# A third token block's u products by rows, a shorter search, and sums held in PSUM in a product-key expert layer

## The chip, the core and the metric

The kernel runs on one core of a Trainium2 chip. The metric is the device time of one execution, in microseconds, as the median of the runs. The core has five engines that matter here: TensorE (PE, with its weight loads as PEld), VectorE (DVE), ScalarE (ACT), GpSimd (POOL) and SyncE (SP), which only issues transfers. 16 DMA engines serve them.

## The reference, cut to what matters

One decoder layer on 1024 tokens of width 1024 in float32. Attention and retention come first and give `h` after a layer norm. The change touches what follows, the product-key experts:

```python
q = (xt @ w_pq).reshape(T, H, 2, 128)              # H = 8 heads
s = einsum('thpd,hpkd->thpk', q, sub_keys)         # 2 x 128 scores a head
s1, i1 = top_k(s[:, :, 0], 16); s2, i2 = top_k(s[:, :, 1], 16)
cand = s1[..., :, None] + s2[..., None, :]         # 16 x 16 sums
top_s, pos = top_k(cand.reshape(T, H, 256), 16)
idx = 128 * i1 + i2 at pos                         # 128 experts a token
g = softmax(top_s)
a = gelu(einsum('cd,ced->ce', x, u[idx])) * g
y = einsum('ce,ced->cd', a, v[idx])
h = layer_norm(ALPHA * h + y, ln2_w, ln2_b)
```

There are 128 x 128 experts, so `u` and `v` have 16384 rows of 1024 numbers.

## The kernel before, in words

The tokens are eight blocks of 128. There are two ways to do the expert sums. **Dense:** multiply by all rows of `u` (or `v`) on TensorE, with a table of gates that is zero where an expert isn't chosen. **By rows:** gather the 128 chosen rows of each token with indirect transfers, and take dot products (`u`) or weighted sums (`v`) on VectorE. `UB = 2` blocks have `u` by rows, `GB = 2` blocks have `v` by rows; the others are dense. Each float32 product is three matmuls on split operands: hi x hi, hi x lo and lo x hi.

`project` (to some 415 us) and `attend` come first. `score` makes the queries and the scores of the heads, and VectorE searches blocks 0 and 1 there; the last head is searched at the start of the next stage.

`experts_in` has 128 tiles of 128 experts. It is written as eight turns (`s`) of 32 slots (`k`); a slot is half a tile. `z_half` (L1093 to L1107) does the dense `u` product of a tile for 768 tokens: 512 in the even slot (`z_first`), 256 in the odd one (`z_rest`), each in 24 matmuls. ScalarE splits the next u tile into its hi part (L795), GpSimd makes the lo part (L799), and ScalarE copies z out (L1175) and stores it. In the same slots, by tables written out by hand:

- `top_piece` (L1249) puts the search of block `s + 2` into the slots of turns 0 to 5, eight pieces for two heads: `side` (16 best of 128), `pairs` (L738: 256 sums, 16 best of them), and for each two heads `names` (L750), which turns positions into expert numbers by comparing with a table of 16 places, two products with the indices and a sum (L758 to L764). `gates` follows in the last slot.
- `gather` (L1209) and `dot` (L1276) do the rows: GpSimd issues one gather for each of 2 x 128 rows, 512 KB each, into a ring of `RING = 3` buffers, `EARLY = 2` ahead; a gather waits until its buffer's row is used. `PER_TURN` (L981) says how many fall in each turn.
- `make_hot` (L1269), `scale_hot`, `gates` and `take_gates` build the gate table of one dense block in each of turns 2 to 7, in 32 steps of four tokens: VectorE makes two hot tiles, ScalarE scales one, TensorE multiplies, ScalarE copies. A hot tile waits until the step two before it is multiplied (L1272). Every gated turn opens with three transposes (L1129), which wait for the search of that block.

All engines run their lists in order, so whatever VectorE has in a slot stands ahead of the next slot's hot tile. SP loads u tiles and scores in one list; the scores wait for the search. In turn 7 it also loads z, gates and v for the next stage.

`experts_out` has 32 rounds (`r`) of four tiles of experts, over six dense blocks (`s`). For each round SP loads z and gates, then the v tiles (L1405 to L1425). ScalarE takes gelu, VectorE multiplies by the gates (L1560), ScalarE and VectorE split that (`a_hi` L1470, `a_lo` L1564) and v (L1475, L1577), TensorE does 12 matmuls for each half block into one of eight PSUM banks in turn (L1443 to L1445), and VectorE adds every bank to `y` in SBUF (`add`, L1567). TensorE waits for the add of eight banks before. 256 gathered v rows are added to blocks 0 and 1 in rounds 1 to 30 (`add_row`, L1550), the two blocks in turn, with four buffers and three ahead. `y` starts as `h` times `ALPHA`, loaded in one transfer of 4 MB (L1419) and scaled in one operation (L1591), both ahead of the first add. `finish` is the norm of a block.

## Time and profile before

| | |
|---|---|
| median of 3 runs | 3082.76 us (3079.69 to 3083.34) |
| the profiled execution | 3082.5 us, span 3080.7 us |
| granted TensorE clock | 0.985 of 2.4 GHz |
| TensorE matmuls | 97% of the span |
| VectorE | 76% |
| ScalarE, GpSimd | 39%, 34% |
| DMA | 693 MB, 225 GB/s in the mean |

The span runs from the first to the last instruction. A busy time is the union of an engine's instructions, so overlapping ones count once. "Idle before" is the time in which the engine stood still ahead of a group, with the work that ended it. A DMA share adds up packet times, and in single stretches it reads above 1.

### The profile page before, as it was taken

The numbers are of one execution on the slowest core, as the hardware profiler recorded it, in microseconds if no ns is written. First come the engines' busy times: TensorE is split into PE (matmuls) and PEld (weight loads), VectorE is DVE, ScalarE is ACT, GpSimd is POOL, SyncE is SP. The second block draws the span as 40 slices with busy tenths as digits, with TensorE's granted clock in tenths as the row PEclk, the third lists the DMA queues.
The fourth block names the chain that finished last, engine by engine and source line by source line (L and its number), as shares of the span: only waits on it lengthen the run. The fifth ranks groups of instructions, "written<-read, shape, count | busy, mean of one in ns | idle before, by whom it ended". The sixth has DMA issues, their size and how long they took to land. (4 is left out here: it accounts for less than half of the span.)

```text
span 3080.7 us, 42384 instructions
## 1 busy us (share of the span) xinstructions
PE 2980.4 (97%) x15866; PEld 2565.9 (83%) x15866; DVE 2327.8 (76%) x4289; ACT 1204.8 (39%) x2245; POOL 1053.0 (34%) x750
## 2 busy tenths in 40 slices
PE   7997998999999999999999999979999999999998
PEld 6887886888888899989898999868888888888887
DVE  4214775567988888888887556569998998999898
ACT  2112332222222566656566657533333333333331
POOL 3222221001455443443434454424433333333331
PEclk9997998999999999999999999989999999999999
DMA  4223222222677666666666888789988898888881
GB/s 169 84 89 123 104 97 83 72 79 69 236 247 255 228 225 234 223 246 241 240 231 250 288 299 301 290 297 317 321 299 302 283 313 292 295 307 296 298 306 74
DMA packets 291846, 693.46 MB, mean 225 GB/s; under 512 B 20304, under 2 KB 134352, under 8 KB 288464
## 3 DMA queue, kind: packets, MB, share of 16 engines
q1 hardware_dynamic: 189776, 315.61, 30.7%
q0 software_dynamic: 73728, 268.47, 24.4%
q10 hardware_dynamic: 28160, 106.96, 9.0%
q8 instruction: 113, 1.85, 0.2%
q14 instruction: 69, 0.57, 0.1%
HBM read 564.08 MB, written 126.88 MB: 224 GB/s over the span
## 5 line engine op out<-in xcount | busy, mean ns | idle before, releaser
L1443 PE MATMUL y_ps<-v_hi,a_hi 128*128 128x512 f32 x1536 | 600.1, 391 | 20.4 <-DVE y L1572 11.5
L1444 PE MATMUL y_ps<-v_lo,a_hi 128*128 128x512 f32 x1536 | 599.6, 390 | 0.0
L1445 PE MATMUL y_ps<-v_hi,a_lo 128*128 128x512 f32 x1536 | 599.4, 390 | 0.0
L799 POOL TENSOR_TENSOR u_lo<-u_raw,u_hi 128x1024 fp32r<-128x1024 f32 x128 | 314.6, 2458 | 725.0 <-ACT u_hi L795 724.0
L1104 PE MATMUL z_first<-hT_hi,u_hi 128*128 128x512 f32 x1024 | 409.9, 400 | 9.5 <-PEq L825 5.1
L1508 POOL DMA_INDIRECT v_rows<-in_v,room x192 | 259.7, 1353 | 463.1 <-DVE y L1555 439.2
L1106 PE MATMUL z_first<-hT_hi,u_lo 128*128 128x512 f32 x1024 | 401.3, 392 | 0.0
L1105 PE MATMUL z_first<-hT_lo,u_hi 128*128 128x512 f32 x1024 | 400.7, 391 | 0.0
L1443 PEld LDWEIGHTS y_ps<-v_hi,a_hi 128*128 128x128 f32 x1536 | 289.6, 189 | 81.6 <-issue 11.9
L1445 PEld LDWEIGHTS y_ps<-v_hi,a_lo 128*128 128x128 f32 x1536 | 289.6, 189 | 60.4
L1444 PEld LDWEIGHTS y_ps<-v_lo,a_hi 128*128 128x128 f32 x1536 | 289.6, 189 | 60.3
L1273 DVE TENSOR_TENSOR hot<-near,iT 128x1024 f32<-128x1024 f32 x192 | 234.1, 1222 | 124.2 <-PE g_ps L1114 122.2
L1572 DVE TENSOR_TENSOR y<-y_ps,y 128x512 f32<-128x512 f32 x384 | 255.2, 685 | 80.9 <-PE y_ps L1445 77.6
L1104 PE MATMUL z_rest<-hT_hi,u_hi 128*128 128x256 f32 x1024 | 297.0, 290 | 0.0
L1105 PE MATMUL z_rest<-hT_lo,u_hi 128*128 128x256 f32 x1024 | 289.7, 283 | 0.0
L1106 PE MATMUL z_rest<-hT_hi,u_lo 128*128 128x256 f32 x1024 | 289.6, 283 | 0.0
L1146 ACT ACTIVATE hot_g<-hot,gT 128x128 f32<-128x128 f32 x768 | 244.4, 390 | 77.7 <-DVE hot L1273 50.0
L1285 DVE CUSTOM_DVE_ANT_0 u_rows<-u_rows,h_ps 128x1024 f32<-128x1024 f32 x170 | 207.3, 1219 | 73.7 <-DMA u_rows<-in_u,room 62.0
L1555 DVE SCALAR_TENSOR_TENSOR y<-v_rows,a_rows,y 128x1024 f32<-128x1024 f32 x192 | 242.5, 1278 | 1.7 <-DMA v_rows<-in_v,room 1.7
L1475 ACT ACTIVATE v_hi<-room 128x1024 fp32r<-128x1024 f32 x128 | 135.4, 1058 | 271.7 <-DMA room<-in_v 267.9
L1104 PEld LDWEIGHTS z_first<-hT_hi,u_hi 128*128 128x128 f32 x1024 | 193.7, 189 | 46.4 <-issue 5.2
L1106 PEld LDWEIGHTS z_first<-hT_hi,u_lo 128*128 128x128 f32 x1024 | 193.3, 189 | 42.5
(195 smaller groups left out, 5829.4 us busy)
## 6 DMA issues: line engine op xcount, KB each, us to landing
u_raw<-in_uT SPq DMA_DIRECT2D x128, 512.0 KB
room<-in_v SPq DMA_DIRECT2D x128, 512.0 KB
z<-z_sb ACTq DMA_DIRECT2D x128, 384.0 KB
gates<-g_sb ACTq DMA_DIRECT2D x24, 2048.0 KB
room<-z SPq DMA_DIRECT2D x16, 1536.0 KB
z_in<-z SPq DMA_DIRECT2D x16, 1536.0 KB
g_in<-gates SPq DMA_DIRECT2D x16, 1536.0 KB
room<-gates SPq DMA_DIRECT2D x15, 1536.0 KB
```

The costliest lines, as they stand in the source:

```text
L799: self.nc.gpsimd.tensor_tensor(self.u_lo[e][:], self.u_raw[e][:], self.u_hi[e][:].bitcast(F32), ALU.subtract).then_inc(self.u_lo_in[e], 1)
L1104: nc.tensor.matmul(o, u_hi[e][:, k], hT_hi[:, k, cols], start=(k == 0), stop=False)
L1105: nc.tensor.matmul(o, u_hi[e][:, k], hT_lo[:, k, cols], start=False, stop=False)
L1106: last = nc.tensor.matmul(o, u_lo[e][:, k], hT_hi[:, k, cols], start=False, stop=(k == KT - 1))
L1146: last = nc.scalar.activation(hot1_g[g][:, t], hot[g][:, 0, t], ACT.Copy, scale=gT[:, t0 + t:t0 + t + 1])
L1273: nc.vector.tensor_tensor(hot[g][:], bc(bc(iota_ps, 1, 4), 1, 2), bc(iT[:, :, t0:t0 + 4], 3, NK), ALU.is_equal).then_inc(hot_in[g], 1)
L1443: nc.tensor.matmul(o, ah, v_hi[p][:, i, c], start=(i == 0), stop=False)
L1444: nc.tensor.matmul(o, ah, v_lo[p][:, i, c], start=False, stop=False)
L1445: last = nc.tensor.matmul(o, al, v_hi[p][:, i, c], start=False, stop=(i == GROUP - 1))
L1508: nc.gpsimd.indirect_dma_start(out=rows_in[i % RING][:], out_offset=None, in_=d["v"].rearrange("a b c -> (a b) c"), in_offset=bass.Indirec ...
L1555: nc.vector.scalar_tensor_tensor(y[:, b], rows_in[i % RING][:], a_rows[:, b, slot:slot + 1], y[:, b], ALU.mult, ALU.add).then_inc(added[b], 1)
L1572: nc.vector.tensor_tensor(y[:, GB + s, c], y_ps[n % 8][:], y[:, GB + s, c], ALU.add).then_inc(y_read, 1)
```

## The change

`UB` goes from 2 to 3: block 2 also has its `u` products by rows, so z has 640 tokens and `z_first` 384 columns. Its `v` product stays dense; its a values enter through the gate table. The third block's last 64 dots of block 1 (`XU = 64`) move to the last stage, which leaves 320 in `experts_in` (`DOTS`) and puts 64 there. The order of blocks in the gate table puts block 2 last.

The search keeps 80 of the 256 sums in four rectangles (those outside can't be among the 16 best), and `decode` works row and column out of a position, for four heads at a time. The pieces of the search go into the first 28 slots of a turn; the names of two pairs of heads stand together after a decode, in every second group of eight pieces. Gathers have six buffers, four ahead; two are the buffers of v, which are loaded later.

In the last stage blocks 0 and 5 of the dense six keep their sums in PSUM over all rounds (`HELD`, four banks), and the other four (`CYCLED`) go back and forth, so that the last of one round is the first of the next and is added once for both; they share four banks. `h` comes in four transfers and is scaled within the first add. The items of the rows are 64 pairs of a v row of block 0 and a u row of block 1, then the rest of block 0, then block 1.

```diff
@@ -32,9 +32,10 @@
 GT = 32
 NG = NK // GROUP
 GB = 2
+XU = 64
 DB = TB - GB
 DT = DB * P
-UB = 2
+UB = 3
 ZB = TB - UB
 ZT = ZB * P
 
...
+    KEPT = [(0, 2, 16), (2, 2, 8), (4, 4, 4), (8, 8, 2)]
...
     def pairs(self, link, b, h):
 
         nc = self.nc
-        link(nc.vector.tensor_tensor(self.cand[:], bc(self.top[:, 0], 2, TOPK), bc(self.top[:, 1], 1, TOPK), ALU.add))
-        self.top16(link, self.cand[:].rearrange("p a b -> p (a b)"), self.cand_left[:],
-                   self.best[:, b % 2, h], self.pos[:, b % 2, h])
+        at = 0
+        for first, n, wide in self.KEPT:
+            part = self.cand[:, at:at + n * wide].rearrange("p (a c) -> p a c", c=wide)
+            last = nc.vector.tensor_tensor(part, bc(self.top[:, 0, first:first + n], 2, wide),
+                                           bc(self.top[:, 1, 0:wide], 1, n), ALU.add)
+            at += n * wide
+        link(last)
+        self.top16(link, self.cand[:], self.cand_left[:], self.best[:, b % 2, h], self.pos[:, b % 2, h])
...
+    def decode(self, link, b, half):
+
+        nc = self.nc
+        pos = self.pos[:, b % 2, half * PH // 2:(half + 1) * PH // 2]
+        row, col = self.ab[:, 0], self.ab[:, 1]
+        link(nc.vector.tensor_scalar(self.step, pos, 4, None, ALU.logical_shift_right))
+        link(nc.vector.tensor_scalar(self.step, self.step, 1, None, ALU.max))
+        nc.vector.tensor_scalar(self.past, self.step, 16, -16, ALU.mult, ALU.add)
+        link(nc.vector.tensor_scalar(self.step, self.step, -1, 5, ALU.mult, ALU.add))
+        link(nc.vector.tensor_tensor(col, pos, self.past, ALU.subtract))
+        link(nc.vector.tensor_tensor(row, col, self.step, ALU.logical_shift_right))
+        link(nc.vector.tensor_tensor(self.past, row, self.step, ALU.logical_shift_left))
+        link(nc.vector.tensor_tensor(col, col, self.past, ALU.subtract))
+
     def names(self, link, b, two):
 
 
         nc = self.nc
         hs = slice(2 * two, 2 * two + 2)
-        pos = self.pos[:, b % 2, hs]
-        nc.vector.tensor_scalar(self.ab[:, 0], pos, 4, None, ALU.logical_shift_right)
-        link(nc.vector.tensor_scalar(self.ab[:, 1], pos, 15, None, ALU.bitwise_and))
-        link(nc.vector.tensor_tensor(self.pick[:], bc(self.ab[:].rearrange("p a h k -> p a (h k)"), 3, TOPK),
+        ab = self.ab[:, :, 2 * (two % 2):2 * (two % 2) + 2].rearrange("p a h k -> p a (h k)")
+        link(nc.vector.tensor_tensor(self.pick[:], bc(ab, 3, TOPK),
                                      bc(bc(self.places[:], 1, 2 * TOPK), 1, 2), ALU.is_equal))
...
-                    if h % 2:
-                        tk.names(link, b, h // 2)
+                    if h % 4 == 3:
+                        tk.decode(link, b, h // 4)
+                        for two in range(2):
+                            tk.names(link, b, h // 4 * 2 + two)
...
-    RING, EARLY = 3, 2
+    RING, EARLY = 6, 4
+    TOPK_SLOTS = 28
+    DOTS = UB * PH * TOPK - XU
     SLOTS = 32
-    PER_TURN = [24, 34, 27, 27, 27, 27, 45, 45]
+    PER_TURN = [40, 40, 34, 34, 34, 34, 60, 44]
     GATE_SLOTS = [SLOTS - 2] * (DB - 1) + [21]
...
-        rows_in = ahead.rows + [sb(f"u_rows{i}", [P, D]) for i in range(RING - len(ahead.rows))]
-        h_own = sb("h_own", [P, D])
-        kept = sb("kept", [P, 3, PH * TOPK])
...
-            first = 6 if s == 0 else 0
-            before, n = sum(PER_TURN[:s]), SLOTS - first
-            return range(before + PER_TURN[s] * max(k - first, 0) // n, before + PER_TURN[s] * max(k + 1 - first, 0) // n)
+            first, end = 6 if s == 0 else 0, 3 * SLOTS // 4 if s == TB - 1 else SLOTS
+            n = end - first
+            at = [sum(PER_TURN[:s]) + PER_TURN[s] * min(max(j - first, 0), n) // n for j in (k, k + 1)]
+            return range(at[0], at[1])
+
+        def pieces_at(k):
+
...
-                    elif n == 2:
+                    elif n == 3:
+                        sp.wait_ge(row_used, DOTS)
                         for e in range(2):
                             sp.dma_start(ahead.v_raw[e][:], d["v"][e]).then_inc(ahead.v_here[e], 16)
-                    elif n == 3:
...
-                    elif n == 6:
+                    elif n == 6 and q % 2:
+                        tk.decode(link, b, q // 2)
+                        tk.names(link, b, q - 1)
+                    elif n == 7 and q % 2:
                         tk.names(link, b, q)
-                    elif n == 7 and q == Q - 1:
-                        v.wait_ge(exps, b + 1)
-                        tk.gates(link, b)
...
-                    tk.names(link, b, PH // 2 - 1)
+                    tk.decode(link, b, 1)
+                    for two in range(Q // 2, Q):
+                        tk.names(link, b, two)
...
-                            top_piece(s, k // 8, k % 8)
+                            for n in pieces_at(k):
+                                top_piece(s, n // 8, n % 8)
+                            if k == TOPK_SLOTS:
+                                v.wait_ge(exps, s + 3)
+                                tk.gates(link, s + 2)
+                                if s + 2 < UB:
+                                    keep_picked(s + 2)
+                                nc.vector.engine_nop().then_inc(found_in, 1)
...
-    ROWS = GB * PH * TOPK
+    SLOTS = PH * TOPK
+    DOT, PLAIN = SLOTS - XU, XU
+    items = [item for n in range(XU) for item in (("v", 0, n), ("u", 1, DOT + n))]
+    items += [("v", 0, n) for n in range(PLAIN, SLOTS)] + [("v", 1, n) for n in range(SLOTS)]
+    ROWS = len(items)
+    of_block = [[i for i, (table, b, _) in enumerate(items) if table == "v" and b == own] for own in range(GB)]
+    dots = [i for i, (table, _, _) in enumerate(items) if table == "u"]
...
+        HELD = (0, DB - 1)
+        CYCLED = list(range(1, DB - 1))
+        LAST = len(CYCLED) - 1
+
+        def order(r):
+
+            if r == 0:
+                return [HELD[0], *CYCLED[:2], HELD[1], *CYCLED[2:]]
+            return [HELD[0], *(CYCLED[::-1] if r % 2 else CYCLED), HELD[1]]
+
+        def run(r, s):
+
+            return LAST * r + (LAST - CYCLED.index(s) if r % 2 else CYCLED.index(s))
+
+        def banks(r, s):
+
+            first = 2 * HELD.index(s) if s in HELD else 4 + 2 * (run(r, s) % 2)
+            return y_ps[first:first + 2]
+
+        def opens(r, s):
+
+            return r == 0 or (s not in HELD and run(r, s) > LAST * r)
+
+        def closes(r, s):
+
+            return r == NG - 1 or (s not in HELD and run(r, s) < LAST * (r + 1))
+
+        def made(r):
...
+                def load_h(blocks, here):
+                    sp.dma_start(y[:, blocks], d["h"].rearrange("n p c -> p n c")[:, blocks]).then_inc(here, 16)
+
                 load_v(0, first=2)
+                load_h(slice(GB + 1, TB - 1), cycled_here)
                 load_z(1)
-                sp.dma_start(y[:], d["h"].rearrange("n p c -> p n c")).then_inc(h_here, 16)
+                load_h(slice(0, GB), rows_here)
                 load_v(1)
+                load_h(slice(GB, GB + 1), held_here)
+                load_h(slice(TB - 1, TB), held_here)
                 sp.dma_start(ln[:, 0], d["ln2_w"]).then_inc(ln_here, 16)
...
-                            wait(pe, y_read, BANKS * r + 2 * s + a - 7)
+                            if s not in HELD and opens(r, s):
+                                wait(pe, y_read, 2 * run(r, s) + a - 3)
...
+                def start_block(b):
+
+                    v.wait_ge(rows_gelu[b], 1)
+                    link(nc.vector.tensor_tensor(a_rows[:, b], a_rows[:, b], ahead.picked_g[:, b], ALU.mult))
+                    link(nc.vector.tensor_scalar(y[:, b], y[:, b], ALPHA, None, ALU.mult))
...
+                def dot_row(i):
+
+                    _, b, slot = items[i]
+                    rows = rows_in[i % RING][:]
+                    v.wait_ge(row_here[i % RING], 16 * (i // RING + 1))
+                    nc.vector.tensor_tensor_reduce(rows, rows, y[:, b], 1.0, 0.0, ALU.mult, ALU.add,
+                                                   ahead.z_rows[:, b, slot:slot + 1]).then_inc(row_used, 1)
...
                 def add(r, s):
+                    held = s in HELD
+                    first = held or r == 0 or (r == 1 and s == CYCLED[-1])
+                    if held:
+                        v.wait_ge(held_here, 32)
+                    elif first:
+                        v.wait_ge(cycled_here, 16)
                     for a in range(2):
-                        n = BANKS * r + 2 * s + a
                         c = slice(a * 512, (a + 1) * 512)
-                        v.wait_ge(y_done, n + 1)
-                        nc.vector.tensor_tensor(y[:, GB + s, c], y_ps[n % 8][:], y[:, GB + s, c], ALU.add).then_inc(
-                            y_read, 1)
+                        part, o = y[:, GB + s, c], banks(r, s)[a][:]
+                        v.wait_ge(y_done, BANKS * r + 2 * order(r).index(s) + a + 1)
+                        if first:
+                            ins = nc.vector.scalar_tensor_tensor(part, part, ALPHA, o, ALU.mult, ALU.add)
+                        else:
+                            ins = nc.vector.tensor_tensor(part, o, part, ALU.add)
+                        ins.then_inc(held_read if held else y_read, 1)
 
                 def split_v(r, i):
                     v.wait_ge(v_hi_in[i % 2], 2 * r + i // 2 + 1)
```

## Rows read from the trace of the kernel before

**Rows 1.** The page: the span, and busy time of TensorE.

```profile
span 3080.7 us, 42384 instructions
...
PE 2980.4 (97%) x15866; PEld 2565.9 (83%) x15866; DVE 2327.8 (76%) x4289; ACT 1204.8 (39%) x2245; POOL 1053.0 (34%) x750
```

**Rows 2.** Busy us of PE, PEld, DVE, ACT, POOL; then clock, DMA share, GB/s.

```profile
883.00:1016.00 133.00, 133.00 (x767) 117.71 (x766) 112.81 (x293) 32.80 (x49) 70.49 (x50) 1.00 0.71 248
...
1179.00:1342.00 163.00, 163.00 (x1029) 147.05 (x1029) 139.97 (x317) 101.41 (x210) 66.24 (x43) 1.00 0.66 236
...
1668.00:1831.00 163.00, 163.00 (x1030) 147.07 (x1029) 94.85 (x131) 101.33 (x209) 81.19 (x62) 1.00 0.79 284
...
2090.00:2998.00 908.00, 908.00 (x4008) 751.85 (x4007) 827.94 (x1026) 302.60 (x448) 322.42 (x240) 1.00 0.88 302
```

**Rows 3.** Single lines of the kernel: first and last start in us.

```profile
L1104 PE MATMUL z_first<-hT_hi,u_hi x1024: 389/389/767, 741.8 to 1995.0; 128*128 128x512 f32 x171
...
L1129 PE MATMUL g_ps<-ident,found x18: 270/271/272, 1021.6 to 1836.9; 128*128 128x128 f32 x18
```

**Rows 4.** Waits in 1179 to 1342 us: total, times, longest.

```profile
DVE hot L1273 <- PE g_ps L1114: 17.6, 9, 3.6
```

**Rows 5.** Timeline of TensorE: start, duration (pipelined).

```profile
1200.05 0.39 PE L1104 MATMUL z_first<-hT_hi,u_hi 128*128 128x512 f32 x1
...
1203.22 0.39 PE L1106 MATMUL z_first<-hT_hi,u_lo 128*128 128x512 f32 x1
...
1204.46 0.28 PE L1105 MATMUL z_rest<-hT_lo,u_hi 128*128 128x256 f32 x1
...
1207.10 0.28 PE L1106 MATMUL z_rest<-hT_hi,u_lo 128*128 128x256 f32 x1
```

**Rows 6.** Groups of VectorE in 1179 to 1342 us: busy, mean ns, idle before.

```profile
L1285 DVE CUSTOM_DVE_ANT_0 u_rows<-u_rows,h_ps 128x1024 f32<-128x1024 f32 x18 | 22.0, 1220 | 1.0 <-DVE top_i L732 0.6
...
L762 DVE TENSOR_TENSOR room<-room,top_i 128x512 f32<-128x512 f32 x8 | 9.3, 1203 | 0.1
...
L731 DVE MAX8 top<-room 128x8 f32<-128x128 f32 x16 | 4.7, 295 | 0.6
...
L728 DVE MAX8 best<-room 128x8 f32<-128x256 f32 x8 | 3.4, 428 | 0.3
```

**Rows 7.** Timeline of VectorE: start, duration.

```profile
762.27 0.18 DVE L756 TENSOR_SCALAR ab<-pos 128x32 uint32<-128x32 uint32 x1
...
762.56 1.23 DVE L758 TENSOR_TENSOR room<-ab,places 128x1024 f32<-128x1024 uint32 x1
...
768.48 0.29 DVE L773 TENSOR_REDUCE gap_sum<-gap_e 128x8 f32<-128x128 f32 x1
...
769.84 0.29 DVE L728 MAX8 top<-s_in 128x8 f32<-128x128 f32 x1
...
1205.68 0.41 DVE L741 TENSOR_TENSOR room<-top 128x256 f32<-128x256 f32 x1
```

**Rows 8.** Groups of VectorE in 2090 to 2743 us, twenty rounds.

```profile
L1555 DVE SCALAR_TENSOR_TENSOR y<-v_rows,a_rows,y 128x1024 f32<-128x1024 f32 x129 | 163.0, 1278 | 1.7 <-DMA v_rows<-in_v,room 1.7
L1572 DVE TENSOR_TENSOR y<-y_ps,y 128x512 f32<-128x512 f32 x243 | 161.8, 685 | 50.3 <-PE y_ps L1445 48.0
```

**Rows 9.** Busy time of each engine in one stretch of 10 us.

```profile
2050.00:2060.00 10.00, 8.19 (x33) 6.41 (x32) 10.00 (x13) 3.25 (x5) 5.47 (x3) 0.92 1.02 380
```

**Rows 10.** Timelines of GpSimd and VectorE: a gather, and its row taken.

```profile
1693.54 0.96 POOL L1215 DMA_INDIRECT u_rows<-in_u,room  x1
...
1698.12 1.22 DVE L1285 CUSTOM_DVE_ANT_0 u_rows<-u_rows,h_ps 128x1024 f32<-128x1024 f32 x1 [3.30 <-DMA u_rows<-in_u,room]
...
2154.24 2.34 POOL L1508 DMA_INDIRECT v_rows<-in_v,room  x1 [3.59 <-DVE y L1555]
...
2163.55 1.28 DVE L1555 SCALAR_TENSOR_TENSOR y<-v_rows,a_rows,y 128x1024 f32<-128x1024 f32 x1 [1.19 <-DMA v_rows<-in_v,room]
```

**Rows 11.** Timeline of VectorE at the start of the last stage.

```profile
2035.67 4.43 DVE L1591 TENSOR_SCALAR y<-y 128x8192 f32<-128x8192 f32 x1 [17.86 <-DMA y<-h]
```

More of the change, by code:

```diff
@@ L265, in __init__ @@
         self.picked_g, self.z_rows = self.carve(UB, PH * TOPK), self.carve(UB, PH * TOPK)
+        self.iota = self.carve(P)
         self.taken = 0
@@ L1370, in experts_out @@
         SKIP = UB - GB
+        DOTS_DONE = next(r for r in range(1, NG) if ROWS * r // (NG - 2) > dots[-1])
+        HELD = (0, DB - 1)
[15 more added lines that the diff above has]
+        def made(r):
+            return order(max(r - 1, 0))
         def tokens(s):
@@ L1607, in _ @@
-                    lo(r, DB - 1)
-                for s in range(DB):
+                        if r > 1 and closes(r - 1, s):
+                            add(r - 1, s)
+                        if n < GROUP:
+                            split_v(r, n)
+                        if n:
+                            lo(r, made(r)[n - 1])
+                        if r == 1 and n == 1:
+                            v.wait_ge(rows_here, 16)
+                            start_block(0)
+                        for i in spread(r, n):
+                            if items[i][0] == "u":
+                                dot_row(i)
+                                continue
+                            if i == of_block[1][0]:
+                                v.wait_ge(row_used, dots[-1] + 1)
+                                start_block(1)
+                            add_row(i)
@@ L1622, in build @@
             tk = TopK(nc, inner, ahead)
-            tiles = ExpertTiles(nc, inner)
+            tiles = ExpertTiles(nc, inner, ahead)
             score(nc, d, hT_hi, hT_lo, tk, tiles, ahead)
```

144 lines of the change are left out of this document (77 added, 67 removed).

## The prediction

> **What bounds the kernel now.** I began with the page. TensorE is busy in 2980.4 of 3080.7 us [rows 1]; its own pace is the time, and the question in every stage is whether another engine is close behind. Next came the busy time by stretch [rows 2]. In the stretches with steps for the gate table, TensorE is busy in all 163 us, VectorE in 140.0 and DMA at 0.66; in the stretch that only takes rows and searches, VectorE is at 112.8 of 133; in the last stage TensorE is at 908 of 908, VectorE at 828, DMA at 0.88. So VectorE stands 10 to 15% behind TensorE, and a large cut of TensorE's work meets it. Third, the ends of the stages: the expert stage begins at 741.8, and the transposes that open each of the six gated turns stand (1836.9 - 0.2 - 1021.6)/5 = 163.0 us apart (0.2 for the third of the last group) [rows 3]. Last, who waits: in a gated turn VectorE waits 17.6 us for TensorE [rows 4], TensorE for nobody.
>
> **Part 1, 128 columns fewer in the dense product.** Fourteen matmuls of 512 columns take 1203.22 - 1200.05 = 3.17 us, 0.226 each; 22 of 256 columns take 2.64, 0.120 each [rows 5]. A line through both puts 384 columns at 0.173, 0.053 less than 512. With 24 such matmuls a tile and 128 tiles TensorE needs 163 us less: 20.4 a turn of 16 tiles. A gated turn would take 142.6; the first two turns, which took 274.4 (741.8 to 1021.6, less 24 x 0.226 for the matmuls ahead of the transposes), would take 233.6. These 163 us come only where the others keep up.
>
> **Part 2, VectorE in the same stage.** (a) Rows: 320 dots in place of 256, by turn 40, 40, 34 x 4, 60, 44 against 24, 34, 27 x 4, 45, 45; one costs 1.22 us [rows 6]. (b) Search: five operations over 80 candidates in place of 256. MAX8 takes 428 ns over 256 and 295 over 128 [rows 6], 1.04 ns an element, so 5 x 176 x 1.04 = 0.92 us less a head. The sum over 256 took 0.41 [rows 7]; four small ones I put at 0.5. Net 0.8 less, 6.6 a turn. (c) Decoding: two operations on 32 positions took 0.29 us [rows 7]; eight, nearly all chained, on 64 positions, I put at 1.7, twice a turn, +3.4; four old pairs go, -1.2. A naming took 762.56 to 768.48, 5.9 us [rows 7]; its two products of 512 elements have a mean of 1203 ns [rows 6], where 512 elements take 685 ns in the last stage [rows 8]: they are held up at times. So a naming is 3.9 to 5.9 us, 4.9 with the mean, and I add 1 for small operations that are held up too.
> A gated turn: 163.0 - 17.6 = 145.4 us without waits; +7 x 1.22 = 8.5, -6.6, +3.4, -1.2, +1 gives 150.5. That is more than TensorE's 142.6. VectorE becomes the bound, and as a decode and two namings (some 12 us) now stand in one slot of 4.5 us, twice a turn, while it may lead TensorE by no more than about a slot, I add 1.5: **152 each**. Four of them: 608 against 652.0, **-44**. Bounds 146 (small operations and locks at half) to 158 (each lump stalls by 4 us more): -68 to -20.
> The first two turns: VectorE's own lead-in is 741.8 to 769.84 [rows 3, 7]; two more namings at 4.9 and two decodes at 1.7, less 2.2 for the shorter search and the old pairs, make the 28 us 39. Then 71 of search (112.8 less 33 dots at 1.30 with their read-out is 70, some 5 of gaps between chained operations, -3.4 as above), 1.2 for a copy and 40 x 1.22 for turn one: 160; 71 + 49 and some 3 of waits for turn two: 123. Together 283 us against TensorE's 233.6. TensorE may not run away: the gathers on GpSimd wait for dots, and the split of the next u tile is queued behind them. Against 274.4 that is +8.6; the first hot tile is wanted two slots into the third turn, which hides 2 to 3: **+6**, bounds -6 (waits and locks at nothing) to +16.
> Turns seven and eight have no search: 32 x 1.22 = 39 of hot tiles and 60 x 1.22 = 73 are 112, below 142.6. Here TensorE keeps its 40.7 us if DMA follows. Turn seven moved 284 GB/s x 163 = 46.3 MB [rows 2]; 15 gathers of 0.524 MB more and a sixth of 6.3 MB of z less make 53.1 MB in 142.6 us, 372 GB/s; with the 44 gathers squeezed into 24 slots of turn eight it is some 378 over 250 us. The best 10 us on record have 380 [rows 9]; the mean of 908 us is 302. I let 95 MB go at 365: +10. **-31**, bounds -41 to -16.
> The Trainium skill (DMA: Bandwidth & Descriptors, Specifications) gives about 358 GB/s as a core's limit to HBM, which speaks against this part. By it these two turns would cost 14 us beyond TensorE's time in place of my 10. The stretch with 380 says that it isn't hard.
>
> **Part 3, the ring.** Six buffers, four gathers ahead; h's own rows and iota move into a larger piece of memory. Costs nothing on the path; v's first tiles are loaded a quarter turn later, with 8 slots still to come. If that cover went, the last stage would start up to 4 us later. In the query stage, names of two pairs fall together once: +1 (0 to +3), as TensorE is fed by VectorE's splits there.
>
> **Part 4, the last stage.** It holds 4608 matmuls in either kernel at 908/4008 = 0.2265 us, 32.6 us a round [rows 2]: nothing to win but at its edges. VectorE per round: 908 busy us are 27.8 rounds, 29.8 each. Six adds fewer (243 took 161.8 [rows 8]): -4.0; one product fewer: -0.7; 320/30 rows in place of 256/30 at 1.26 (163.0/129): +2.7; rows of one block now follow each other, each waiting for the one before, some 0.15 each by the chained operations [rows 7]: +1.6. 29.4: no worse. TensorE now reuses a bank two runs later, not four blocks later, so an add must be done within a block's 24 x 0.2265 = 5.44 us; VectorE waits at that point today, so it fits. DMA: 302 x 32.6 = 9.86 MB a round, +1.12 -0.26: 10.7 MB, 328 GB/s. A gather has from the end of the row four back to its own turn, 10.9 - 1.5 = 9.4 us with two rows in a block. One in turn seven took 4.57 us (1693.54 to 1698.12), the one that VectorE waited for in the last stage 9.31 (2154.24 to 2163.55) [rows 10]. Most lie below 9.4: **+3**, bounds 0 to +45.
> The start: all of h (4 MB) held VectorE idle until 2035.67, then 4.43 us of scaling [rows 11], and TensorE waited for the first bank. Now the cycled blocks come first, but VectorE still meets v of the next group ahead of its first add, some 8 MB after 2003; at 302 GB/s that is 27 us, with a split behind it near 2033. **-8**, bounds -12 to 0. The tail has the same six norms: 0.
>
> **Sum.** 3082.5 +1 +6 -44 -31 +3 -8 = 3009.5, **3009 us**. The execution traced took 3082.5 beside a median of 3082.8, so no shift.
>
> **Rivals.**
> *TensorE stays the bound throughout.* For it: it is so in every stage today, and VectorE has 17.6 us of waits a turn. Against it: the sum of 150. It gives 3082.5 - 163 - 8 = 2912; half of it, 2958, if small operations cost half.
> *DMA becomes the bound.* If no more than 316 GB/s can be held, 5% over the 302 of now [rows 2], a round takes 10.7/316 = 33.9 us, +38 in thirty, and turns seven and eight cost 15 more: 3062. For: the demand of 372. Against: 380 in single stretches.
> *Slower: gathers in the last stage come too late.* Period of a block with two rows is (latency + 1.5)/2 once that exceeds 5.44, so it decides from 9.4 us, and the gain is gone at 10.3. At 10.7 it is 6.1 us, 36.6 a round, +119: 3128. For: 9.31 is on record and the load rises. Against: only 1.19 us of wait came of it.
> *The cut doesn't shorten the matmul*, weight loads being the floor: 256 columns run at 0.120, so 384 can't be held at 0.226. VectorE's 150 would fit below 163 again, and 3082.5 - 8 + 4 = 3078 would be left.
>
> **Numbers.** Forecast 0.71, TensorE throughout (or near it) 0.08, DMA 0.13, late gathers 0.07, no shorter matmul 0.01. If all bounds fell together they would be -127 and +20; the parts are largely independent, so 2960 to 3050 holds 8 in 10, with the halves of the first and second rivals that lie near it. Within 0.2% (what can be told from no change) lies little: 0.03; slower 0.07, faster 0.90.
>
> **What will show it.** Right: gated turns 150 to 154 us apart, TensorE waiting for hot tiles or gates in them, VectorE over 95% busy; the third turn beginning near 1022; turns seven and eight near 147; rounds of 32.6 us. Wrong: gated turns at 143, or above 160; rounds above 33; VectorE waiting for rows in the last stage by more than 50 us.

## The result and the profile after

| | before | after |
|---|---|---|
| median of 4 runs | 3083.05 us (3079.69 to 3084.41) | 3038.14 us (3037.21 to 3044.0) |
| ratio after to before | | 0.9861 (95%: 0.9846 to 0.9875) |
| span of the profiled execution | 3080.7 us | 3042.1 us |

The change saves 45 us, 1.4%. The forecast was 3009, a gain of 73: the sign is right and the time inside the range, but 28 us of the gain didn't come. The stages tell where. A turn's start is that of its first `z_first` matmul, every 16th tile in TensorE's timeline; a round is 144 matmuls of the last stage.

| us | before | after | difference | forecast |
|---|---|---|---|---|
| start of the expert stage | 741.8 | 743.8 | +2.0 | +1 |
| turns 1, 2 | 140.9, 133.4 | 159.9, 122.0 | +7.6 | +6 |
| turns 3 to 6 | 162.9, 163.0, 163.0, 163.0 | 158.5, 157.5, 156.7, 156.8 | -22.4 | -44 |
| turns 7, 8 | 163.0, 167.3 | 144.9, 149.6 | -35.8 | -31 |
| end of turn 8 to the last stage | | | -1 | 0 |
| rounds 0 and 1 | 48.2, 36.4 | 44.3, 47.4 | +7.1 | -8 |
| rounds 2 to 31 | 32.64 each | 32.64 each | 0 | +3 |
| from TensorE's end to the span's | 11.0 | 15.0 | +4 | 0 |

In the last line VectorE is done at 3035.1 and the span ends 7.0 us later, with the last store; before it was 3.0 us. That isn't chance: ten of the eleven kernels below, all but that of experiment 8, also take 15 us from TensorE's end to the span's. What makes the 4 us isn't shown. Besides, the profiled execution took 5.9 us more than the median (the other three have spans of 3035.3 to 3036.7), and which stage holds these can't be read from one trace.

Windows of the kernel after, as in [rows 2]: busy us of PE, PEld, DVE, ACT, POOL; clock, DMA share, GB/s. They are turn 1, turn 2, a gated turn, turns 7 and 8, and the last stage.

```profile
744.00:904.00 160.00, 121.48 (x769) 120.46 (x770) 150.27 (x437) 32.06 (x52) 77.42 (x57) 0.86 0.68 232
904.00:1026.00 122.00, 115.83 (x769) 115.43 (x770) 113.83 (x343) 31.20 (x49) 78.13 (x58) 0.98 0.87 294
1184.00:1342.00 158.00, 146.54 (x1033) 145.82 (x1033) 144.18 (x364) 99.64 (x210) 72.14 (x50) 0.96 0.75 263
1655.00:1800.00 145.00, 142.96 (x1030) 141.87 (x1030) 108.98 (x154) 100.43 (x211) 93.24 (x75) 1.00 0.96 359
1800.00:1950.00 150.00, 144.45 (x1030) 142.38 (x1028) 96.13 (x132) 100.02 (x214) 76.14 (x57) 1.00 0.88 332
2048.00:2960.00 912.00, 912.00 (x4025) 755.19 (x4024) 781.89 (x942) 289.83 (x421) 378.77 (x298) 1.00 0.93 325
```

In turn 1 TensorE now stands idle for a quarter of the time. In a gated turn it is busy for 146.5 of 158 at a clock of 0.96, where before it was busy throughout at 1.00: neither engine is full, which is the mark of two that stop each other. In the last stage it is still full. The waits in turn 1 and in that gated turn (total, times, longest):

```profile
PE z_first L1139 <- POOL u_lo L823: 38.5, 5, 17.2
```

```profile
PE g_ps L1149 <- ACT hot_g L1181: 10.3, 2, 5.2
PE g_ps L1149 <- ACT g_sb L1192: 1.1, 1, 1.1
...
DVE hot L1308 <- PE g_ps L1149: 6.3, 6, 4.0
DVE iT L1348 <- PE g_ps L1164: 1.4, 1, 1.4
```

VectorE waits 6.3 us for TensorE where it waited 17.6 [rows 4], and TensorE, which waited for nobody, waits 10.3 in two stops. One of them in VectorE's timeline (start, duration), then GpSimd's and TensorE's at the same place:

```profile
1241.00 1.23 DVE L1308 TENSOR_TENSOR hot<-near,iT 128x1024 f32<-128x1024 f32 x1 [0.42 <-PE g_ps L1149]
1242.14 0.42 DVE L765 TENSOR_SCALAR step<-pos 128x64 uint32<-128x64 uint32 x1
...
1244.25 1.22 DVE L780 TENSOR_TENSOR room<-ab,places 128x1024 f32<-128x1024 uint32 x1
...
1248.10 3.27 DVE L780 TENSOR_TENSOR room<-ab,places 128x1024 f32<-128x1024 uint32 x1
1251.40 1.29 DVE L784 TENSOR_TENSOR room<-room,top_i 128x512 f32<-128x512 f32 x2
1252.73 1.22 DVE L786 TENSOR_REDUCE found<-room 128x64 f32<-128x1024 f32 x1
1253.98 1.22 DVE L1320 CUSTOM_DVE_ANT_0 room<-room,h_ps 128x1024 f32<-128x1024 f32 x1
...
1255.13 1.22 DVE L1308 TENSOR_TENSOR hot<-near,iT 128x1024 f32<-128x1024 f32 x1
```

```profile
1247.90 2.39 POOL L823 TENSOR_TENSOR u_lo<-u_raw,u_hi 128x1024 fp32r<-128x1024 f32 x1 [4.10 <-ACT u_hi L819]
```

```profile
1257.71 2.08 PE L1149 MATMUL g_ps<-hot_g,hot 128*128 128x128 f32 x8 [5.06 <-ACT hot_g L1181]
1259.44 0.67 PE L1139 MATMUL z_first<-hT_hi,u_hi 128*128 128x384 f32 x1
1259.91 0.52 PE L1140 MATMUL z_first<-hT_lo,u_hi 128*128 128x384 f32 x1
...
1261.47 0.33 PE L1139 MATMUL z_first<-hT_hi,u_hi 128*128 128x384 f32 x1
```

Between two hot tiles lie 14.1 us: a decode (2.1), a naming (3.85), a second one (5.9, its first operation held for 3.27 in place of 1.22 while GpSimd's split runs until 1250.3) and a dot. This run of work between two hot tiles is called a lump below. TensorE stands for 5.06 us and then works at 0.32 to 0.5 us a matmul, the lower clock of 1.2 GHz, until 1261.4; then at 0.17. So the stop costs more than its wait. The 0.17 also confirms part 1: 384 columns take the forecast 0.173.

VectorE went into this lump as far ahead as it may be. Its hot tile of 1241.00 had to wait for TensorE, and it was multiplied 6.5 us after it was ready; no tile of this turn waits much longer. The tile behind the lump was multiplied 1.4 us after it was ready, the time that ScalarE takes to scale it. The turn can then be added up from TensorE's side: 142.6 of its own work (part 1), 11.4 of waits, and about 2 lost to the low clock after each of two stops (matmuls are slow for 3.8 and 4.1 us) are 157.9, and it took 157.5.

At the start of the last stage, TensorE's waits between 1954 and 2060 us, and the end of the longest in VectorE's timeline:

```profile
PE y_ps L1529 <- DVE a_lo L1671: 18.7, 2, 12.6
PE y_ps L1529 <- DVE y L1686: 6.7, 1, 6.7
```

```profile
2011.74 0.68 DVE L1671 TENSOR_TENSOR a_lo<-z_in,a_hi 128x512 fp32r<-128x512 f32 x1
...
2013.48 1.28 DVE L1654 SCALAR_TENSOR_TENSOR y<-room,a_rows,y 128x1024 f32<-128x1024 f32 x1
2016.62 1.23 DVE L1662 CUSTOM_DVE_ANT_0 v_rows<-v_rows,y 128x1024 f32<-128x1024 f32 x1 [1.85 <-DMA v_rows<-in_u,room]
...
2017.77 0.69 DVE L1671 TENSOR_TENSOR a_lo<-z_in,a_hi 128x512 fp32r<-128x512 f32 x1
```

Block 4 is the last of round 0 and the second of round 1. Its `a_lo` (2017.77) is made in VectorE's list behind round 1's row items, which wait for gathers, and TensorE starts on it at 2018.5 after 12.6 us.

VectorE's waits in rounds 2 to 31 (2048 to 2994 us):

```profile
DVE y L1654 <- DMA v_rows<-in_v,room: 52.9, 45, 2.9
DVE y L1688 <- PE y_ps L1531: 38.6, 29, 2.0
DVE v_rows L1662 <- DMA v_rows<-in_u,room: 21.9, 17, 2.6
DVE y L1654 <- DMA room<-in_v,room: 14.0, 15, 2.1
```

88.8 us of waits for rows, 77 times, none over 2.9, and every round stays at 32.64.

### The profile page after: what moved, and what is told of

It is laid out like the page before. It is cut to its first block and busy times, and to the rows that moved or that the text cites. A ratio compares the mean times of both kernels' runs of the same rounds, so it can differ in the third digit from the quotient of the medians.

```text
span 3042.1 us, 42759 instructions
## 1 busy us (share of the span) xinstructions
PE 2836.2 (93%) x15866; PEld 2542.9 (84%) x15866; DVE 2315.9 (76%) x4590; ACT 1172.3 (39%) x2215; POOL 1167.8 (38%) x878
## 5 line engine op out<-in xcount | busy, mean ns | idle before, releaser
L823 POOL TENSOR_TENSOR u_lo<-u_raw,u_hi 128x1024 fp32r<-128x1024 f32 x128 | 308.0, 2406 | 612.9 <-ACT u_hi L819 612.6
L1139 PE MATMUL z_first<-hT_hi,u_hi 128*128 128x384 f32 x1024 | 360.5, 352 | 49.7 <-POOL u_lo L823 44.7
L1599 POOL DMA_INDIRECT v_rows<-in_v,room x176 | 235.6, 1339 | 340.4 <-DVE y L1654 323.4
L1140 PE MATMUL z_first<-hT_lo,u_hi 128*128 128x384 f32 x1024 | 350.9, 343 | 0.0
L1141 PE MATMUL z_first<-hT_hi,u_lo 128*128 128x384 f32 x1024 | 350.1, 342 | 0.0
L1654 DVE SCALAR_TENSOR_TENSOR y<-v_rows,a_rows,y 128x1024 f32<-128x1024 f32 x176 | 225.6, 1282 | 58.5 <-DMA v_rows<-in_v,room 54.6
L1149 PE MATMUL g_ps<-hot_g,hot 128*128 128x128 f32 x1536 | 210.9, 283 | 50.4 <-ACT hot_g L1181 43.5
L1149 PEld LDWEIGHTS g_ps<-hot_g,hot 128*128 128x128 f32 x1536 | 197.9, 197 | 56.0 <-ACT hot_g L1181 45.8
L1139 PEld LDWEIGHTS z_first<-hT_hi,u_hi 128*128 128x128 f32 x1024 | 200.1, 195 | 51.3 <-POOL u_lo L823 46.1
L1320 DVE CUSTOM_DVE_ANT_0 room<-room,h_ps 128x1024 f32<-128x1024 f32 x161 | 196.3, 1219 | 33.3 <-DMA room<-in_u,room 21.4
```

The lines of the kernel that those rows point to most:

```text
L823: self.nc.gpsimd.tensor_tensor(self.u_lo[e][:], self.u_raw[e][:], self.u_hi[e][:].bitcast(F32), ALU.subtract).then_inc(self.u_lo_in[e], 1)
L1139: nc.tensor.matmul(o, u_hi[e][:, k], hT_hi[:, k, cols], start=(k == 0), stop=False)
L1140: nc.tensor.matmul(o, u_hi[e][:, k], hT_lo[:, k, cols], start=False, stop=False)
L1141: last = nc.tensor.matmul(o, u_lo[e][:, k], hT_hi[:, k, cols], start=False, stop=(k == KT - 1))
L1149: last = nc.tensor.matmul(g_ps[g][:, t], hot[g][:, 1, t], hot1_g[g][:, t], start=True, stop=True)
L1599: nc.gpsimd.indirect_dma_start(out=rows_in[i % RING][:], out_offset=None, in_=d["u"] if table == "u" else d["v"].rearrange("a b c -> (a b) ...
```

## The experiments

Every kernel starts from the changed one. A time of one run can be off by some 4 us (the four runs above span 7); ratios are to the kernel before, with a 95% interval. The kernel before took 3080.5 to 3082.0 us beside them and 3083.1 beside the changed kernel, so a difference between medians taken at two times can be off by 2 or 3 us more.

### 1. The second naming apart from the first

```diff
                     elif n == 6 and q % 2:
                         tk.decode(link, b, q // 2)
                         tk.names(link, b, q - 1)
-                    elif n == 7 and q % 2:
-                        tk.names(link, b, q)
+                    elif n == 6 and q:
+                        tk.names(link, b, q - 1)
...
                             if k == TOPK_SLOTS:
+                                tk.names(link, s + 2, Q - 1)
```

> The changed kernel with one thing moved: the second naming of each decode leaves the slot of the first (the pair of heads 2 and 3 is named in piece 6 of the third group, that of heads 6 and 7 in slot 28). Same instructions, other places. Theory A (the lumps): a gated turn takes 157 us because VectorE's 13 us lump makes TensorE stand still 5 us twice and run at half clock after it; VectorE's own work without waits is 149.8. With lumps halved the turns of 157 fall to 150 to 152, TensorE's waits for hot_g from 10 us a turn to under 3, the first turn (160) and the second (122) together by 0 to 8, the whole by 22 to 35 us: 3005 to 3018. Theory B (the bound is VectorE's sum with the lock that GpSimd holds, and lumps only place the waits): gated turns stay within 2 us of 157, the whole within 8 us of 3038.

3021.26 us (3019.37 to 3023.69), ratio to the kernel before 0.9808 (0.9792 to 0.9824), 17 us faster than the changed kernel. Gated turns 157.1, 153.7, 152.5, 152.6, turn 2 115.5. TensorE's waits for `hot_g` fall from 10.3 us a turn to 6.2 (here in 1184 to 1342 us):

```profile
PE g_ps L1149 <- ACT hot_g L1181: 6.2, 3, 5.8
```

The first six turns take 20.5 us less (7 of them in turns 1 and 2), and round 1 gives 2 back (49.7). So the place of the naming alone was worth 17 us, less than theory A expected and more than theory B: gated turns stop at 152.5. The lump in the middle of the turn is gone, the one at its end is not, and it still stops TensorE for 5.8 us. In the third gated turn VectorE waits for TensorE at 1385.2 and then not again for 90 us. Its lead goes from 6.5 to 1.4 us in this time, and the last lump meets a lead of 1.8 where it had met 4.9.

### 2. No row items in round 1

```diff
-            return range(ROWS * max(r - 1, 0) // (NG - 2), ROWS * r // (NG - 2)) if r < NG - 1 else range(0)
+            return range(ROWS * max(r - 2, 0) // (NG - 3), ROWS * max(r - 1, 0) // (NG - 3)) if r < NG - 1 else range(0)
...
```

Two more lines, which follow from this one, are left out.

> The changed kernel, with the row items of the last stage in rounds 2 to 30 and none in round 1 (320 items over 29 rounds, 11.0 a round in place of 10.7). Theory A: in round 1 TensorE waits 12.6 us for an a_lo, because the block that stands last in round 0 stands second in round 1, and its a_lo is made behind the rows of that round on VectorE; without rows there the wait is under 3 us, round 1 takes 34 to 38 us in place of 47.4, and the whole 9 to 13 us less (3025 to 3029). Theory B: the wait comes from the late v tiles of the next group (18.6 us of waiting for them on ScalarE), rows or none; then round 1 stays at 44 us or more and the whole within 4 us of 3038. Both: later rounds stay at 32.6.

3026.0 us (3023.26 to 3028.24), ratio 0.9825 (0.9809 to 0.9842), 12 us faster. Round 1 takes 32.64 in place of 47.4, round 0 44.8; the wait for `a_lo` of 12.6 is gone. The rows in round 1 were the cause, and the later rounds carry them without loss.

### 3. The first 216 dots on a quarter of their columns

```diff
-                    nc.vector.tensor_tensor_reduce(rows_in[r][:], rows_in[r][:], h_ps[:], ...
+                    w = D // 4 if i < sum(PER_TURN[:6]) else D
+                    nc.vector.tensor_tensor_reduce(rows_in[r][:, 0:w], rows_in[r][:, 0:w], h_ps[:, 0:w], ...
```

It leaves out three quarters of each of those dot products; the transfers stay.

> Leaves work out: the first 216 dots (turns 1 to 6) multiply only 256 of the 1024 columns, the gathers stay whole. That takes some 0.8 us from each dot on VectorE, 32 us from turns 1 and 2, 27 from each gated turn. Theory A (VectorE is the bound of the first six turns): gated turns fall from 157 to TensorE's 142.6 to 145, the first two from 282 to 240 to 252, the whole by 75 to 95 us: 2945 to 2965. Theory B (GpSimd, DMA or ScalarE hold them): they fall by less than half of that.

2996.17 us (one run). Turns 1 and 2 take 137.2 and 112.9, 32 us less; the gated turns 153.8, 153.8, 153.7, 155.2, only 13 less in four, though VectorE has 30 us less to do in each (windows and waits in 1165 to 1318 us):

```profile
1165.00:1318.00 153.00, 144.64 (x1024) 143.95 (x1023) 114.91 (x361) 98.11 (x209) 72.48 (x50) 0.98 0.77 269
```

```profile
PE g_ps L1149 <- ACT hot_g L1181: 8.4, 2, 4.3
...
DVE hot L1308 <- PE g_ps L1149: 27.6, 21, 4.3
```

VectorE waits 27.6 us in the turn and TensorE still stops twice, behind each lump. Turn 2 falls to TensorE's own pace (112.5 by the forecast's 0.173 and 0.120 us a matmul), so VectorE's work held it. A gated turn is held at 153.8 by the lumps even when VectorE's sum is 30 us smaller.

### 4. Both: names apart, quarter dots

The edits of 1 and 3 together, leaving out the same.

> Leaves work out: as in the quarter-dot run, the first 216 dots multiply 256 of 1024 columns; and the namings stand apart. Quarter dots alone left the gated turns at 153.8 us with VectorE busy only 115, namings apart alone at 152.5 to 154 with VectorE at 142 to 144. Theory A (two limits, each near 153 by itself: VectorE's sum, and a lump longer than its lead over TensorE): with both taken away gated turns fall to 143 to 146 and the whole to 2950 to 2970. Theory B (a third thing, ScalarE's order or the gate banks, holds TensorE at 153): they stay above 150.

2945.78 us (one run). Gated turns 143.2, 143.5, 143.2, 143.2; TensorE waits 0.5 us for `hot_g` and its clock is 1.00:

```profile
1130.00:1273.00 143.00, 141.89 (x1025) 141.11 (x1024) 114.47 (x363) 98.66 (x210) 71.65 (x50) 1.00 0.81 290
```

So both have to go. Small sum and lumps as they were: 153.8. Namings apart and the sum as it was: 152.5, with one stop. With neither, TensorE's 142.6 of the forecast is nearly reached, and theory B is out. That the lumps are a limit by themselves is shown by experiment 3. That the sum is one by itself isn't shown, as no run has a full sum and no stop; what experiment 1 shows is that a full sum leaves VectorE no lead with which to meet the last lump.

### 5. Add and store the dense sums in every round

```diff
-            return r == 0 or (s not in HELD and run(r, s) > LAST * r)
+            return True
...
-            return r == NG - 1 or (s not in HELD and run(r, s) < LAST * (r + 1))
+            return True
```

All eight banks are used in turn, and `h` of two blocks is loaded ahead of v.

> The changed kernel without sums held in PSUM: every block is added to y in every round (384 adds in place of 198), in eight banks in turn as before; h's last two blocks are loaded ahead of v. Theory A: VectorE is busy 28.0 us a round and waits 3.1 for rows; six more adds at 0.67 are 4.0, 35 us against TensorE's 32.6, so rounds take 34 to 35.5 and the whole is 40 to 85 us longer, 3080 to 3120: the held sums pay for the 64 dots there. Theory B: waits for rows shrink as VectorE gets later, and rounds stay at 32.6 to 33; the whole stays within 10 us.

3041.61 us (one run). Window 2100 to 2900 us and VectorE's first waits in it, here and then in the changed kernel:

```profile
2100.00:2900.00 800.00, 798.94 (x3521) 659.96 (x3520) 766.21 (x967) 249.18 (x364) 337.84 (x260) 1.00 0.94 323
```

```profile
DVE y L1653 <- DMA v_rows<-in_v,room: 12.5, 22, 1.4
DVE y L1687 <- PE y_ps L1531: 5.6, 7, 1.2
```

```profile
2100.00:2900.00 800.00, 800.00 (x3531) 662.43 (x3530) 685.32 (x825) 252.37 (x367) 333.65 (x262) 1.00 0.94 325
```

```profile
DVE y L1654 <- DMA v_rows<-in_v,room: 45.7, 40, 2.9
DVE y L1688 <- PE y_ps L1531: 32.2, 24, 2.0
```

VectorE is busy 81 us more of 800 and most of its waits vanish, but TensorE loses 1 us, and 2.5 over rounds 2 to 31; round 1 takes 51.0, 3.5 more. The waits for rows were VectorE's spare time. Holding sums in PSUM is worth 3 to 6 us here at most, about what two single runs can differ by; the order in which `h` is loaded changed with it.

### 6. Three buffers, two gathers ahead in the last stage

```diff
-    RING, EARLY = 4, 3
+    RING, EARLY = 3, 2
```

> The changed kernel with three row buffers and two gathers ahead in the last stage, in place of four and three. With two rows in a block the time from a buffer's release to its next use falls from 9.4 us to 5.3, below the 7 us of a gather. Theory A (the late gathers of the prediction): VectorE waits some 2 us a block more, 8 to 10 a round, and rounds take 34 to 38 us: the whole 3080 or more. Theory B: VectorE has 4 us to spare and TensorE's banks hide the rest, rounds 32.6 to 33.2, the whole under 3055.

3092.87 us (one run), slower than the kernel before. Rounds take 32.6 to 37.1, round 1 52.8:

```profile
2100.00:2900.00 800.00, 771.85 (x3350) 633.05 (x3349) 647.04 (x783) 234.54 (x349) 294.34 (x248) 0.99 0.91 308
```

```profile
DVE y L1654 <- DMA v_rows<-in_v,room: 80.5, 53, 4.0
DVE y L1654 <- DMA room<-in_v,room: 41.9, 27, 5.3
```

This is the rival of late gathers, one buffer away. The core moves fewer bytes a second (308 GB/s against 325) and VectorE waits more, so it is the time of a single gather that binds and not the rate. In the changed kernel a gather of this stage lands 8.0 us after its issue in the median (4.2 to 11.6).

### 7. Both moves

The edits of 1 and 2 together.

> Both moves together: namings apart and no rows in round 1. They touch different stages, so their gains of 17 and 12 us should add: gated turns 153 to 154, round 1 at 32.6, the whole 3006 to 3013. If it is over 3018, one takes from the other, by the DMA load at the start of the last stage.

3002.92 us (3000.87 to 3004.67), ratio 0.9745 (0.9729 to 0.9761): 35 us faster than the changed kernel, with nothing left out. The medians' gains of 17 and 12 make only 29; by the stages of the traces the first six turns give 21 and rounds 0 and 1 give 15, and round 1 no longer loses the 2 us of experiment 1. Turns 159.5, 115.4, 157.1, 153.7, 152.5, 152.5, 144.1, 147.6; rounds 44.0 and then 32.64.

### 8. Both moves, 96 dots in the last stage

```diff
-XU = 64
+XU = 96
...
-    PER_TURN = [40, 40, 34, 34, 34, 34, 60, 44]
+    PER_TURN = [40, 40, 32, 32, 32, 32, 60, 20]
```

> The two moves, and 96 dots in place of 64 in the last stage, 12.1 row items a round; gated turns have 32 dots each, turn 8 has 20. Theory A (a dot costs 1.22 us where VectorE is the bound, and the last stage has some 4 us a round left, as adding in every round showed): gated turns 2.4 us shorter, turn 8 by 2 to 3, rounds at 32.6 still; 10 to 13 us under the run with both moves. Theory B (DMA, 340 GB/s wanted there): rounds rise above 33 and it is slower than that run.

3026.14 us (3025.73 to 3031.04), ratio 0.9828 (0.9812 to 0.9844), 23 slower than experiment 7. Turn 8, with 24 rows fewer, gains 4.2; rounds take 32.6 to 36.7, 33.7 in the mean. A gated turn with two dots fewer stays at 152.5. The traces show where the 2.4 us go in the third one: 1.2 into the four small sums of the search, which are held up longer (10.6 us for 9.4), and 1.3 into VectorE's wait for the transposes at the turn's head (3.4 for 2.1). The stop behind the last lump is 5.8 us as before.

```profile
2100.00:2900.00 800.00, 784.86 (x3422) 638.78 (x3421) 704.44 (x863) 245.21 (x358) 372.41 (x289) 1.00 0.97 337
```

```profile
DVE y L1655 <- DMA v_rows<-in_v,room: 36.1, 40, 2.9
DVE y L1655 <- DMA room<-in_v,room: 27.0, 24, 2.7
```

TensorE loses 15 us of 800. VectorE is busy for only 704 and doesn't wait for TensorE at all: the rest of its time goes to rows that aren't there (24.2 more for rows of u). Their supply is the bound, at 337 GB/s and a DMA share of 0.97. Whether that is the rate or again the time of one gather isn't separated: where VectorE waited, a row was used 8.9 us after its issue in the median, against 8.7 in experiment 7, and now 12.1 of them are wanted a round for 11.0. Of the two counts tried, 64 dots cost this stage nothing and 96 are too many.

### 9. All 256 sums again

```diff
-    KEPT = [(0, 2, 16), (2, 2, 8), (4, 4, 4), (8, 8, 2)]
+    KEPT = [(0, 16, 16)]
```

The decode goes back to two operations.

> The changed kernel, but each pair searches all 256 sums again and the position is decoded by two operations; everything else stays. Nothing is left out. By durations of the two traces the search costs 0.8 us more a head (8 a turn), the decode 1.8 us less, twice a turn: VectorE's sum is 6.4 - 3.6 = +2.8 us a turn. Theory A (VectorE's sum and its lumps both count, and the shorter decode makes the lump 1.8 us shorter): gated turns 157 to 160 us, first two turns together 3 to 10 us longer, total 3040 to 3055 beside 3038. Theory B (only the lump counts in the gated turns): gated turns 154 to 156, total 3030 to 3038. Theory C (the compressed search was worth what was put down for it, 6.6 us a turn, with the decode hidden): gated turns 163 or more, total 3070.

3040.59 us (one run). Turns 161.3, 122.2, 158.0, 156.4, 156.0, 156.8: within 2 us of the changed kernel's everywhere. The shorter search is worth nothing that this run can show. The traces show why it could be worth little. In the third gated turn, 1341.7 to 1498.4 us in the changed kernel and 1341.6 to 1497.7 here, the sums cost this (the first two lines are the changed kernel's):

```profile
L749 DVE TENSOR_TENSOR room<-top 128x16 f32<-128x16 f32 x24 | 5.0, 261 | 0.0
L749 DVE TENSOR_TENSOR room<-top 128x32 f32<-128x32 f32 x8 | 1.6, 201 | 0.0
...
L749 DVE TENSOR_TENSOR room<-top 128x256 f32<-128x256 f32 x8 | 3.5, 434 | 0.0
```

The five searching operations take 9.6 us a turn in place of 16.9, as forecast; but the four small sums take 6.6 in place of 3.5, and the decodes 3.8 in place of 0.8, inside the lumps. VectorE is busy for 142.6 us of the one turn and 143.4 of the other. That the decode's place in the lump takes the rest was not tried apart.

### 10 and 11. The last lump taken further apart

With both moves one stop of 5.8 us is left in a gated turn, at its end. The first try put decode and naming into pieces 6 and 7, and the last naming and the gates into slot 29:

> On top of both moves (names apart, rows late), the last lump of a gated turn is taken apart too: the decode keeps its slot, the first naming goes one slot behind it, and the naming of the last pair goes with the gates from slot 28 to slot 29. Nothing is left out. In the kernel with both moves a gated turn took 152.5 to 153.7 us, TensorE waited 5.8 us once a turn (at 1467.45, behind a decode, a naming with 3.50 us in its products, and a dot) and two dots fewer gave nothing. Theory A (that one stop is what is left of the bound; VectorE's own sum is 152.5 - 1.8 - 2.0 = 148.7 us): gated turns 148.5 to 150.5 from the second on, TensorE's longest wait for hot_g under 3 us, total 2989 to 2997 us. Theory B (VectorE's sum is the bound and the stop only where it shows): gated turns stay at 152 to 153.7, total 3000 to 3006. Theory C (the gates, one slot later, make TensorE's transposes wait): a new wait of 2 to 4 us at the end of a turn, total 3000 to 3015.

3005.81 us (3004.04 to 3007.03), gated turns 158.1, 154.3, 153.1, 153.1, a stop of 5.75 at the same place. Pieces 6 and 7 fall in one slot (27), so it separated nothing. The second put the decode into slot 27, a naming into each of 28 and 29:

> The run before, with decode and naming apart, separated nothing: the two pieces it put apart fall in the same slot (27), and only the gates and the last naming moved. Here they are apart in fact at the end of a gated turn: on top of both moves, slot 27 holds the decode alone, slot 28 the naming of the third pair, slot 29 that of the fourth and the gates. Nothing is left out. Theory A (the one stop of 5.8 us a turn, behind decode, naming, dot in slot 27, is what holds 152.5 to 153.7; VectorE's own sum is 148.7): gated turns from the second on 148.5 to 151, the longest wait for hot_g in such a turn under 4 us, total 2989 to 2999 us. Theory B (VectorE's work in slots 27 to 29 together is the lump, wherever the cut between the slots; two namings and a decode come in 14 us of TensorE's pace either way): gated turns 152.5 to 154, a wait of 5 us or more still there, total 3001 to 3008. Theory C: transposes wait for the gates, 2 to 4 us a turn more.

3001.9 us (3001.06 to 3004.19), ratio 0.9743 (0.9726 to 0.9759), not to be told from experiment 7. Gated turns 155.7, 154.1, 154.0, 152.6. Waits of TensorE in 1340 to 1492 us, in experiment 7 and here:

```profile
PE g_ps L1149 <- ACT hot_g L1181: 6.0, 2, 5.8
```

```profile
PE g_ps L1149 <- ACT hot_g L1181: 6.5, 4, 4.3
```

The wait is in four pieces and in total no smaller. Theory B fits: what counts is all that VectorE does in slots 27 to 29, which it enters with a lead of 1.8 us in either kernel (hot tile 27 of the turn). Fewer dots near the end of the turn, or a third hot buffer, would test this and weren't tried.

## Why the prediction was right, and where it was wrong

**Part 1** held: 0.17 us a matmul of 384 columns in the timeline, and 143.2 us a turn where nobody holds TensorE (experiment 4) against the forecast 142.6.

**First two turns** held: +7.6 for +6. The third turn begins at 1025.7 (forecast 1022), and experiment 3 shows VectorE's work as the cause. In part this is luck: experiment 1, with the same work in other places, takes 7 us off these two turns, and the forecast had no term for that here. TensorE's wait is seen at `u_lo`, 38.5 us in turn 1, as the forecast had it (the split queued behind gathers that wait for dots).

**Gated turns** are the step that failed: "+1.5" for the lumps. VectorE's own sum is as forecast, 157.5 - 6.3 - 1.4 = 149.8 against 150.5; what I added for the lumps should have been 157.5 - 149.8 = 7.7. They lay outside the 150 to 154 named as the sign of "right", and VectorE was busy for 91% of a turn and not for over 95%. The forecast saw decode and two namings in one slot of 4.5 us, and still took the turn for VectorE's sum with a little on top. But the lump is a limit of its own: two of them hold a turn at 153.8 with 30 us less of VectorE's work (experiment 3). With the namings apart and the full sum one stop is left and the turn takes 152.5 (experiment 1); with both taken away it takes 143.2 (experiment 4). So what a turn costs is TensorE's own time and its stops, and the sum works through the lead that VectorE has when a lump comes. After a stop TensorE also runs at half clock for some 4 us, which the forecast didn't price: about 2 us each. The upper bound of 158 in the forecast was right, and this is where the value lay: 157.4 for 152, four times, is 21.6 us of the 28.6. The credit of 6.6 us a turn for the shorter search was too large: beside experiment 9 it is 4.2, as four small sums cost 0.82 us a head and not 0.5. With its decode it bought nothing that shows.

**Turns 7 and 8** held: -35.8 for -31. Turn 7 moved 359 GB/s over 145 us and took 144.9, 2 us above TensorE's pace; turn 8 took 149.6, and in experiment 8 it was 4.2 shorter with 24 rows fewer. The Trainium skill's limit of about 358 GB/s (DMA: Bandwidth & Descriptors, Specifications) would have given a loss of 14 and measured is 294.5 - 285.2 = 9.3; the mean of turn 7 lies at that figure, and the 371 GB/s of one slice of the page lies above it.

Slices of the page after (GB/s in 40 slices of 76 us):

```profile
GB/s 163 93 88 129 105 87 70 81 73 83 217 278 302 267 262 259 270 262 262 265 261 270 361 371 362 268 321 315 333 329 314 325 335 312 326 337 310 331 324 70
```

**The start of the last stage** failed, in its sign: -8 for rounds 0 and 1, measured +7. The first round did gain 4. But the forecast followed `h` and v and never asked which block comes second in round 1: with the order going back and forth it is the one whose a values VectorE makes last, now behind row items that wait for fresh gathers. Experiment 2 gives it all back: rounds 0 and 1 then take 77.4, 7.2 less than before, for the forecast 8. It is 15 us against the forecast.

**The last stage** held: 32.64 a round. The sign named for "wrong", waits for rows above 50 us, came (88.8) without the loss. A wait of an engine with 130 us to spare in 912 is no cost, and experiment 5 turns it into work for 3.5 us. The better sign would have been that VectorE no longer waits for TensorE: it waited 32.2 us of 800 here, 3.3 in experiment 6 and not at all in 8, where TensorE lost 28 and 15. The rival of late gathers is real at one buffer fewer (3093); at 32 dots more (3026 for 3003) it is late gathers or the DMA rate. The time of a gather fits the last stage only just, 8.0 us in the median where the forecast allowed 9.4.

Between the forecast and the profiled execution, 3044.0 - 3009.5 = 34.5 us, lie +21.6 (gated turns), +15.1 (rounds 0 and 1), +4 (after TensorE's end), -4.8 (turns 7 and 8), -3 (later rounds), +1.6 (turns 1 and 2), +1 (score stage) and -1 (the change of stages), which makes 34.5. The median is 5.9 lower, 28.6 above the forecast.

Two numbers of the prediction don't come out of its own terms. The upper bounds of the parts add up to +28, not +20. The DMA rival lets 95 MB go at 316 GB/s, which takes 301 us where the forecast had 260: turns 7 and 8 would cost 41 us more, not 15, and the rival's time would be near 3088, not 3062. Neither changes the forecast.

## What to carry to other kernels

A term "X fits into the slot on average" needs a second one for each lump longer than the lead that the buffers allow, and where both engines are nearly full, the stop is paid in full and some more in clock. Spread such work before it is made shorter: moving one naming gave 17 us, the smaller search nothing that shows. When a loop's order is turned round, list for the second trip which input is made last. And a helper's waits for data are no warning while it still waits for the main engine as well.

## What I hadn't expected of the hardware

A VectorE operation on two SBUF operands was held until a GpSimd split had ended: 3.27 us in place of 1.22 (at 1248.10, split until 1250.29), and 3.50 for two products that take 1.29 (experiment 7, at 1458.93, split from 1459.17 to 1461.89). The Trainium skill (SBUF — State Buffer, Who interferes with whom) says that a VectorE instruction with two SBUF inputs contends with a GpSimd instruction that reads SBUF, and the traces agree.

After each stop of TensorE that I looked at, of 4.1 us (experiment 3) to 12.6, its granted clock was the lower one, 1.2 GHz. Windows of the kernel after around three of them, in rounds 0 and 1 of the last stage (the clock is the third figure from the end):

```profile
1954.00:1961.00 7.00, 4.96 (x12) 3.85 (x13) 4.80 (x6) 4.18 (x7) 4.26 (x4) 0.52 0.76 259
1985.00:1992.00 7.00, 4.79 (x12) 3.81 (x13) 6.69 (x10) 4.73 (x8) 0.00 (x0) 0.51 0.41 140
2009.00:2022.00 13.00, 3.49 (x8) 2.81 (x9) 9.05 (x12) 3.22 (x5) 5.64 (x5) 0.50 1.04 377
```

The core held 359 GB/s for 145 us with gathers of single rows in the mix, and 377 for 13 us.
